# Between the second mixer and the experts: residuals ahead of a split by halves, later second weights, sooner selections, three count products

## The reference

```python
        y = jnp.concatenate([y_conv, y_att], axis=-1) @ w_out[l]
        x = x + g1[:, None, :] * y
        h = modulate(rmsnorm(x, norm_ffn_g[l]), sh2, sc2)
...
    logits = (t @ w_router).astype(jnp.float32) + b_router.astype(jnp.float32)
    top_val, top_idx = lax.top_k(logits, TOP_K)      # TOP_K = 2 of N_EXPERTS = 8
    top_w = jax.nn.softmax(top_val, axis=-1)
...
    for e in range(N_EXPERTS):
        out = out + combine[:, e:e + 1] * swiglu(t, w_gate[e], w_up[e], w_down[e])
```

## Time and profile before

| what | value |
|---|---|
| time, median of 3 runs | 2195.18 us (2194.23 to 2195.26) |
| the profiled execution's own time | 2193.78 us |
| its span | 2191.9 us |
| TensorE busy | 2126.7 us, 97% of the span |
| VectorE, ScalarE busy | 1773.1 us, 1380.5 us |
| moved by DMA | 574.89 MB, 262 GB/s on average |

### The profile page before, as it was taken

The page is one execution under the profiler, slowest core; times in us unless marked ns, Lnnn a source line. Parts: engine busy times, 40 slices in busy tenths (PEclk is TensorE's granted clock), DMA queues, the critical chain, the costliest instruction groups (busy, mean ns, idle before and its releaser), DMA issues.

```text
span 2191.9 us, 31299 instructions
## 1 busy us (share of the span) xinstructions
PE 2126.7 (97%) x12762; PEld 1875.5 (86%) x12762; DVE 1773.1 (81%) x2269; ACT 1380.5 (63%) x1962; POOL 2.1 (0%) x16
## 2 busy tenths in 40 slices
PE   7999999999999999999988999999999999999998
PEld 7899999899998889999887888878888787887876
DVE  5778886788888757767847888898988889888987
ACT  4555544655547654446746777777767777777775
POOL 0000000000000000000000000000000000000000
PEclk9999999999999999999998999999999999999999
DMA  5357684357684317765316999889988999999984
GB/s 189 119 201 278 231 301 155 137 190 271 233 317 154 114 58 291 255 208 208 116 58 256 365 359 346 344 340 364 366 333 336 353 362 344 347 350 344 370 344 183
DMA packets 89429, 574.89 MB, mean 262 GB/s; under 512 B 10048, under 2 KB 10048, under 8 KB 31040
## 3 DMA queue, kind: packets, MB, share of 16 engines
q1 hardware_dynamic: 87984, 566.89, 69.4%
q0 software_dynamic: 288, 3.15, 0.4%
q10 hardware_dynamic: 1008, 2.79, 0.3%
HBM read 571.75 MB, written 1.05 MB: 261 GB/s over the span
## 4 chain that ended last, share of the span: by engine, by line
PE 84%; DVE 10%; ACT 3%; DMA 1%; issue 1%; DVEq 0%; ACTq 0%
PE bank L2005 42%; PE bank L483 41%; DVE wlo L1373 2%; DVE arena L1764 1%; PE bank L2063 1%; DVE RSTD L1439 1%; DVE extra_lo L1373 1%; ACT whi L995 0%; DMA ring<-in_w_in 0%; ACT hT L1038 0%; DVE XC L1448 0%; ACT extra_hi L995 0%; DMA side<-in_w_ada 0%; DVE XC L1428 0%; DMA cst<-in_cst 0%
## 5 line engine op out<-in xcount | busy, mean ns | idle before, releaser
L1373 DVE TENSOR_TENSOR wlo<-ring,whi 128x1024 fp32r<-128x1024 f32 (+1 forms) x766 | 878.1, 1176 | 138.6 <-ACT whi L995 129.2
L995 ACT ACTIVATE whi<-ring 128x1024 fp32r<-128x1024 f32 (+1 forms) x766 | 759.9, 1020 | 213.0 <-PE bank L483 128.8
L483 PE MATMUL bank<-HH,whi 128*128 128x256 f32 x1536 | 442.1, 288 | 7.2 <-DVE HL L1488 5.3
L483 PE MATMUL bank<-HH,wlo 128*128 128x256 f32 x1536 | 435.0, 283 | 0.0
L483 PE MATMUL bank<-HL,whi 128*128 128x256 f32 x1536 | 434.1, 283 | 0.0
L483 PEld LDWEIGHTS bank<-HH,whi 128*128 128x128 f32 x1536 | 293.5, 191 | 11.6 <-DVE HL L1488 6.4
L483 PEld LDWEIGHTS bank<-HL,whi 128*128 128x128 f32 x1536 | 293.7, 191 | 1.0 <-issue 0.5
L483 PEld LDWEIGHTS bank<-HH,wlo 128*128 128x128 f32 x1536 | 293.5, 191 | 0.0
L1373 DVE TENSOR_TENSOR extra_lo<-ring,extra_hi 128x1024 fp32r<-128x1024 f32 x224 | 264.2, 1219 | 14.8 <-ACT extra_hi L995 14.5
L995 ACT ACTIVATE extra_hi<-ring 128x1024 fp32r<-128x1024 f32 x224 | 229.9, 1060 | 53.4 <-PE bank L2005 53.4
L2005 PE MATMUL bank<-whi,xg 128*128 128x512 f32 x672 | 221.1, 397 | 0.0
(11 more groups left out here) (291 smaller groups left out, 3527.9 us busy)
## 6 DMA issues: line engine op xcount, KB each, us to landing
ring<-in_moe_gate SPq DMA_DIRECT2D x112, 1024.0 KB, 5.2
ring<-in_moe_up SPq DMA_DIRECT2D x112, 1024.0 KB, 6.3
ring<-in_moe_down SPq DMA_DIRECT2D x112, 1024.0 KB, 5.1
side<-in_w_ada SPq DMA_DIRECT2D x96, 512.0 KB, 4.2
ring<-in_w_up SPq DMA_DIRECT2D x44, 1024.0 KB, 4.9
ring<-in_w_in SPq DMA_DIRECT2D x32, 1024.0 KB, 4.9
ring<-in_w_down SPq DMA_DIRECT2D x32, 704.0 KB, 4.6
ring<-in_ffn_gu SPq DMA_DIRECT2D x22, 1024.0 KB, 4.9
```

What stands on the lines that cost most here:

```text
L483: return pe.matmul(out, lhsT, rhs, start=start, stop=stop, skip_group_check=True)
L995: a.activation(hi, part, ACT.Copy).then_inc(*made.up(("hi", n, i)))
L1373: v.tensor_tensor(lo, part, hi.bitcast(F32), ALU.subtract).then_inc(*done.up(("lo", n, i)))
```

## The change

Four things are edited. (1) On VectorE, in the last chunk `c` = 3 of `w_out2` of either layer, tile 6's residual comes ahead of the split; in layer 1 that split is cut in two: half 0 between the residuals of tiles 6 and 7, half 1 behind the normalization. On ScalarE, in layer 1 only, half 0 comes behind tile 6's square and half 1 behind tile 7's. (2) The split of `first_moe + 1` moves on ScalarE behind the four row copies, on VectorE behind the low parts of the rows. (3) `select(0)` and `select(1)` move from the routed program to a place between `icnt` and the second half of the low rows. (4) The five small count products become three, of which two write 16 columns.

```diff
-            mm(b[:, 0:8], C("earlier"), msk[:, 0, :], True, True)
-            mm(b[:, 8:16], C("earlier"), msk[:, 1, :], True, False)
-            mm(b[:, 8:16], ones, msk[:, 0, :], False, True)
-            mm(b[:, 16:24], ones, msk[:, 0, :], True, False)
+            mm(b[:, 0:16].rearrange("p (i e) -> p i e", i=2), C("earlier"), msk, True, False)
+            mm(b[:, 8:24].rearrange("p (i e) -> p i e", i=2), ones, msk[:, 0, :].unsqueeze(1).broadcast_to([128, 2, 8]), False,
+               False)
             mm(b[:, 16:24], ones, msk[:, 1, :], False, True).then_inc(*p_rout.up(("counts",)))
...
@@ act_program, for c in range(4)
-                    if c > 0:
+                    last = (l, c) == (1, 3)
+                    if c > 0 and not last:
                         ahead(CH["w_out2", l, c])
                     for k in (2 * c, 2 * c + 1):
                         norm_tile(N["rms1", l], k)
+                        if last:
+                            split(first_moe, (k - 6,))
                 rms_modulated(1, l)
                 if l == 1:
-                    split(first_moe + 1)
                     break
...
                     a.activation(HNH[:, i, 512 * g:512 * g + 512], PS[BANK["hn", i, g]][:, :], ACT.Copy).then_inc(
                         *a_rout.up(("hn", i, g)))
+            split(first_moe + 1)
...
+        def select(v, e):
+            v.wait_ge(*v_rout("pos"))
+            v.wait_ge(*a_norm(("rms1", 1), "dst", 7))
             for i in range(2):
+                v.tensor_scalar(PSEL[:, i, e, :], iota, pos[:, i, e:e + 1], None, ALU.is_equal).then_inc(*r_vec.up(("select", e)))
...
@@ dve_program, for c in range(4)
-                    if c > 0:
+                    if 0 < c < 3:
                         ahead(CH["w_out2", l, c])
                     for m in range(2):
+                        if (c, m) == (3, 1):
+                            split(first_moe, (0,)) if l else ahead(CH["w_out2", l, c])
...
                 rms_modulated(1, l)
                 if l == 1:
-                    split(first_moe + 1)
+                    split(first_moe, (1,))
                     break
...
             v.tensor_copy(icnt[:, :], cmx).then_inc(*v_rout.up(("count",)))
+            for e in range(2):
+                select(v, e)
             low_of_rows(1)
+            split(first_moe + 1)
...
@@ dve_routed
-            select(0)
-            select(1)
             for g in range(4):
                 gather(0, g)
```

More of the change, by code:

```diff
@@ L984, in at_of, with act_split @@
                     return u, S_all[:, u, kw * i:kw * i + kw]
-        def act_split(a, n, used=p_w, made=a_hi):
+        def act_split(a, n, used=p_w, made=a_hi, halves=range(2)):
             a.wait_ge(*ARRIVED[n])
-            for i in range(2):
+            for i in halves:
                 hi, _, part, before = HALVES[n, i]
@@ L997, in act_program, with split @@
         def act_program(a):
-            def split(n):
-                act_split(a, n)
+            def split(n, halves=range(2)):
+                act_split(a, n, halves=halves)
             def ahead(n):
@@ L1364, in act_program, with dve_split @@
                         *a_rout.up(("hn", i, g)))
-        def dve_split(v, n, made=a_hi, done=v_lo):
+            split(first_moe + 1)
+        def select(v, e):
+            v.wait_ge(*v_rout("pos"))
+            v.wait_ge(*a_norm(("rms1", 1), "dst", 7))
             for i in range(2):
+                v.tensor_scalar(PSEL[:, i, e, :], iota, pos[:, i, e:e + 1], None, ALU.is_equal).then_inc(*r_vec.up(("select", e)))
+        def dve_split(v, n, made=a_hi, done=v_lo, halves=range(2)):
+            for i in halves:
                 hi, lo, part, _ = HALVES[n, i]
@@ L1375, in dve_program, with split @@
         def dve_program(v):
-            def split(n):
-                dve_split(v, n)
+            def split(n, halves=range(2)):
+                dve_split(v, n, halves=halves)
             def ahead(n):
@@ L2179, in ahead @@
                     dve_split(v, n + 2, made=r_hi, done=moe_lo["r"])
[L2181 to L2186, removed]
             def gather(p, g):
@@ L2235, in dve_routed @@
                     if 0 < n < NE - 1:
-                        select(n + 1)
+                        select(v, n + 1)
                     if f == 2 and e > 0:
```

## The result

The changed kernel took 2183.4 us (median of 6 executions, 2182.7 to 2184.46) against 2194.92 us of the kernel before (6 executions, 2192.79 to 2195.26): a ratio of 0.995, 95% interval 0.9937 to 0.9963, so 8 to 14 us less. The profiled execution took 2183.72 us, with a span of 2181.9; 2184.8 was forecast for it.

A forecast was written before the change was run, and what follows sets the result against it. TensorE, busy 97% of the span, bounds the kernel, so only its holes count. Terms 3.90 + 2.54 + 1.35 + 1.19 = 8.98, so 9.0 us off a median of 2195.18: 2186.2 us, range 2184.4 to 2188.6.

The forecast's parts named there:

- layer 0: Layer 0's last output chunk: earlier residual 6 and later split cancel, 0 us, bounds ±0.3.
- A: Layer 1's norm: with reordered residuals and split halves the root starts at 1145.46, not 1149.36; 3.90 us, bounds 3.7 and 4.0.
- B: Router's end to logits: logits no longer wait for VectorE's second split, 2.54 us.
- C: Count products: six passes at full clock, then VectorE's low rows decide; 1.35 us, or 0.92 at low clock.
- D: Counts to first gather: it waits for the small instructions and four selections, 1.48 us in place of 2.67; 1.19 us gained.
- gather to slot weights: After the gather's start: low rows and second split delay VectorE's copies, with one microsecond to spare; 0 us.
- The clock sentence: Before the counts: TensorE rests 2.4 us in place of 4.95, more than half at full clock, so counts run there.
- The branch: Rival: register load and branch exposed before the gather, up to 1.2 us later, 2187.4 us; 0.18 together with a later clock rise.
- the clock rise later: Rival in the gather: 16 more passes at low clock cost 1.8 us, 2188.0 us; 0.18 together with the exposed branch.
- The clock through the gather: Rival: clock stays up through the gather, VectorE's third copy then sets the slot weights; gain 10.1, 2185.1 us; chance 0.14.
- The experts ate nothing: Rival: the experts are set by transfers, so starting them early gives nothing, 2195 us; chance 0.04.
- Chunk 7: Rival: weight chunk 7, issued behind the moved split, lands 25 us late and the kernel is slower, 2200 us; chance 0.02.

The follow-up runs named there:

- w_old: The kernel before, run again with no edit: median 2194.81 us, ratio 1.0001 to before.
- w_again: The changed kernel, run again with no edit: median 2185.78 us of 5 executions, ratio 0.996 to its kernel before.
- w_third: The changed kernel, run a third time with no edit: median 2184.29 us of 5 executions, ratio 0.9954 to its kernel before.
- w_fill: The changed kernel with filler products on TensorE, two between the transposes and the counts, three behind the counts: median 2185.62 us of 4 executions.
- w_second: The kernel before with only the second split moved, behind ScalarE's row copies and VectorE's low rows: median 2194.68 us, ratio 1.0001.

## Why the prediction was right or wrong

| step | forecast | before to after | with the repeats |
|---|---|---|---|
| layer 0 | 0 | 0 | 0 |
| A, the norm | 3.90 | 4.13 | 4.29 |
| B, logits | 2.54 | 2.56 | 2.57 to 2.58 |
| C, counts | 1.35, bounds 0.92 and up | 0.85 | 1.32 to 1.33 |
| D, selections | 1.19 | 1.18 | 1.19 |
| gather to slot weights | 0 | 0.12 | 0.49 |
| sum | 8.98 | 8.84 | 9.86 to 9.88 |

The first measured column is before less after, the second w_old less w_again and w_third. B and D follow from the edits alone; A, C and the last step also carry what clock each execution drew.

**Layer 0** was right. Tile 7's square moved there from 810.45 to 808.36, by 2.09 us, but all around it had moved as far: tile 5's residual of layer 0, ahead of the edit, by 2.08 (803.91 to 801.83), and the root by 2.08 (811.64 to 809.56). From the table load near 781 us to the one near 822 it is 39.76 to 40.27 us in 12 of the 14 traces, with the edit or without; the two others are before (41.18) and w_fill (41.08), one of either kind.

**A** was right in mechanism, and 0.2 to 0.4 us small, outside its stated bounds of 3.7 and 4.0. I let each instruction start when the one ahead had ended; in the rows the root starts at 1144.18 while half 1 runs to 1144.27. (The forecast's own steps also put the end of half 1 at 1145.50 and not at 1145.46, a slip of 0.04.) The rest is clock: in w_old, the same program as before, the root waited for a slower sum and came 0.16 us later (12.01 to 11.85).

**B** and **D** were right. **C** had the right pair of values, and the launch draws which: 1.42 us of passes at the lower level in the first trace (0.85, just under the bound of 0.92), 0.81 at the upper in w_again and w_third (1.32 to 1.33), where VectorE's low rows then decide, as worked out. This is w_again's, in TensorE's and in VectorE's timeline:

```profile
1158.43 0.81 PE L483 MATMUL bank<-small,cst 128*128 128x16 f32 x6 [0.99 <-DVE small L1918]
```

```profile
1158.20 1.28 DVE L1885 TENSOR_TENSOR HL<-bank,hnh 128x512 fp32r<-128x512 f32 x2
1159.40 0.17 DVE L1922 SCALAR_TENSOR_TENSOR small<-bank,small 128x16 f32<-128x16 f32 x1
```

The clock sentence that went with it failed: TensorE rested 1.2 us and not 2.4, since the transposes took 3.14 us for the 1.94 of the trace before, and the clock fell in them while the engine was busy.

**The step that failed** is in the sum's last lines. "The median is 1.4 above it" took the distance between one traced execution and the median of three others for a property of the kernel and added it to the forecast of the traced execution. After the change the median lies 0.3 below the traced execution, so this term alone is 1.7 us of the 2.8 between 2186.2 and 2183.4. The other 1.1 us are in the traced execution itself (2184.8 forecast, 2183.72 measured), and 1.05 of them lie ahead of tile 5's residual, where only the edit of layer 0 stands, which gave 0, and for which the prediction had no term. The range gave all of this "half a microsecond of spread", and the same program's executions reach from 2182.70 to 2187.87.

The terms had a small share. They give 9.0, the stretch measured 9.4 us on average (37.85 for the two traces of the kernel before, 28.41 for three of after): A and the gather's clock were too small, C in the first trace too large. In the first pair of traces alone they come out at 8.84 for 8.98, and that is partly luck: A gave 0.23 more, C 0.50 less, the last step 0.12 more. What is left of 11.5 beyond 9.4 is luck too, as far as the records show: the clock that the executions drew, 3.5 us between single traces ahead of tile 5, and 2.4 us between three medians of one program, of which 2183.4 is the lowest. With all three the gain is 8.8 to 11.0 us by the ratios. A range for a median of five or six launches would have had to reach about 1.5 us to either side beyond the terms' own, an estimate from these three medians. Why one group of launches draws a higher clock than another is open. The chip they ran on is a possible reason that no run tests; the two chips with both versions on record don't order them alike (before 2194.52 and 2195.7, after 2185.78 and 2184.29).

**The rivals.** The branch was hidden, but with 0.01 us to spare, so its chance was fairly given. Nor did the clock rise later relative to the work: from gather to slot weights it is 6.35 to 6.39 us in the three traces of the kernel after, and 6.51 and 6.84 before. The clock through the gather was not up by itself; w_fill shows that the rival's mechanism was right, third copy and all. The experts ate nothing: the rest is 1016.55 to 1017.07 in all traces. Chunk 7 was not late: in the kernel after its transfer is issued at 1162.25 and its first split starts at 1178.99, after a wait of 0.39 us for TensorE and not for the transfer, as at 1188.90 in the kernel before.

## What to carry to other kernels

Where an engine's queue holds a long piece of work that is not needed yet ahead of a short one that is, put the short one first and cut the long one so that its parts fill holes; but move all that stands in the same queue, since a split moved by itself (w_second) only waits further down. Read a term by the events around it, counted from the last event that no edit moves: where the clock draws alike this repeats to 0.02 us (28.24 and 28.22), where it doesn't to 0.5 (28.76), and medians of eleven launches don't resolve 1. And give the range of a median the spread of the launches, not that of the sum, and don't carry the distance from one execution to a median over from one kernel to the next.

## What the runs showed of the hardware

Register load and branch cost TensorE 0.86 us together, the hop included. The clock fell while TensorE was busy: in the kernel after it was at full level through the router's products (1.00 from 1147.70 to 1151.50), 0.59 on average over the transposes with 3.17 of 3.20 us busy. Identical programs had stages at 0.87 and at 1.00 of the clock, 1.7 us apart. Where it doesn't need the result of the one ahead, an instruction of ScalarE or VectorE starts some 0.08 us before that one's recorded end (1143.23 + 1.04 and 1144.18 on ScalarE, 1157.83 + 0.15 and 1157.90 on VectorE).
